# A two-layer decoder step: where the first mixer loads its sample states and exponential table, and the order of the second mixer's weight transposes

## The chip, the cores and the metric

The kernel runs on one core of one Trainium2 chip. The metric is the device time of one execution in microseconds (us); lower is better. The time before is the median of three runs.

## The reference, cut to what matters

One inference step of a two-layer decoder with width 1024 works on a prompt of 1024 tokens and on a group of 8 samples with 4 tokens each (1056 tokens in all). Everything is float32.

```python
# layer 0
proj = rmsnorm(h) @ w_in_a                       # q, k (8 heads x 64), v, o (8 x 128), two gates
h_mix, (c, n, m) = mlstm_chunkwise(q, k, v, ...) # chunks of 128 tokens, state c 64 x 128, n 64, m per head
h = h + (sigmoid(o) * rmsnorm_per_head(h_mix)) @ w_out_a
h = h + square(relu(rmsnorm(h) @ w_up[0])) @ w_down[0]
# layer 1
k, v = rmsnorm(h) @ w_kv                         # 16 heads x 64, samples also read 1024 old rows from a paged cache
z = (q @ k.T) * 64**-0.5 + bias
log1mb = where(mask, log_sigmoid(-z), 0)         # stick-breaking: a = sigmoid(z) * prod of (1 - sigmoid) of later keys
a = exp(where(mask, z + reverse_cumsum(log1mb), -inf))
h = h + (a @ v) @ w_out_b
h = h + square(relu(rmsnorm(h) @ w_up[1])) @ w_down[1]
y = rmsnorm(h)
```

The samples begin their mLSTM from given states; their new states and the prompt's last state are outputs, as are the new keys and values.

## The kernel before, in words

The residual stream `h` stays on the chip, feature by token. A float32 product of the dense layers is made of three products of split operands: a high and a low part each of weights and activations, low by low left out. GpSimd (POOL) splits each 128-column weight panel, SyncE's queue (SP) loads it. The 1056 tokens are three tiles of 352 columns. The program is a row of phases with their own semaphores: constants, embedding, the first mixer (`mixer_a`), output projection and MLP, the second mixer (`mixer_b`), output projection and MLP, the final norm. Each engine's order is written out by hand.

**The first mixer** works on the 8 heads in 4 pairs. For a pair, a list of items (`PLANS[p]`, from `items_of`) sets one order for PE, ACT and DVE: `u` (PE spreads the gate sums over the partitions at L741 and L743; ACT makes decay weights of them with Exp at L908), `k` and `v` (PE transposes, L730, ACT copies the rows, L934), `wsp`, `scores`, `dc` (state additions of the prompt), `out` (the previous pair's heads are transposed back, L723), `num` (numerators, copied by ACT at L944), `dcs` (state additions of the samples). Between the items PE works on thirds of the projection tiles of the next pair (L703 to L705), so many as `FILL` says; for the last pair few are left. An `u` item on PE waits until ACT has made the decay weights of the `u` before it, since both use bank 2.

The loop of ACT over the pairs begins at each pair with the load of the **next** pair's sample states: it waits for the present pair's states to be in, and from pair 1 on also for the stores of the pair before (`state_out`), since the two state tiles alternate. `load_state` then issues two DMAs from ACT's own queue, L871 for the matrices and L872 for the normalisers. Behind the items, `squares(p)` applies Sigmoid to the output gates (L952) and squares the numerators (L959, L960); then ACT issues four stores from its queue (L990 to L993), the last of which writes the samples' normalisers, 4 KB of single elements. In the second item of the next pair `inverse_rms` forms the per-head inverse root with Ln (L964) and Exp (L966). DVE then scales the heads (L1169).

ACT evaluates its functions from a table that must be loaded (`ACT_TABLE_LOAD`). The compiler places a load ahead of a function that the present table lacks. The program asks for the table `natural_log_exp_and_others` by name once, at its start (L2011); the first norm's Ln (L315) and Exp (L318) ran without a load of their own behind it, in the later norms each had one.

**The second mixer** works on 16 heads in 8 pairs, and each pair in 8 slots, one for each prompt tile of 128 queries, from tile 7 down to tile 0 (`TILE_AT`). A tile's keys stand in chunks: for tiles 7 to 4 an upper one (keys from 512 on, `x = 0`) and a lower one (keys 0 to 511, `x = 1`), for tiles 3 to 0 one. For each chunk and head PE makes scores (`z`, L1443 and L1447), ACT the two sigmoids (`gates`, L1627 and L1628), DVE a reversed running product (L1770) and the weights (L1776, `a_ready`). The gates of a tile's first chunk wait until DVE has finished the tile before. Slots 0 and 4 of a pair also hold DVE's chain of the samples (L1782, L1785), ahead of the tile's own.

One slot after a tile, PE transposes its weights in packs of two 128-key blocks with two heads each (L1491), ACT copies a pack to SBUF (L1681), and PE multiplies it with the values into bank 7 (L1536); an odd tile number has an even number of blocks, an even one a last pack of one block. The packs, other transposes (`turn`), the thirds of the next pair's projections (L1427 to L1429) and the quarters of the samples' values (L1550) follow one another as `turns` says; the lower chunk's scores come behind the second turn. ACT reads the turns in the same order, with the upper gates ahead of them. The eight tiles `a` form a ring; ACT may write one again when the pack that reads it last has been transposed.

Of the kernel before, what the change touches and what calls it, by code (L numbers as in the profile page):

```python
# [513 lines left out]
def mixer_a(nc, m, own):  # L514

    HP = HA // 2
# [58 lines left out]
    with ExitStack() as c:  # L575
# [287 lines left out]
        def _(act):  # L863
# [104 lines left out]
            for p in range(HP + 1):  # L968
                if p + 1 < HP:
                    act.wait_ge(state_in, 32 * (p + 1))  # L970
                    if p:
                        act.wait_ge(state_out, 64 * p)
                    load_state(p + 1)
                for i, (x, _) in enumerate(PLANS[p]):
                    if x[0] == "u":
                        decay(x)
                    elif x[0] in ("k", "v"):
                        rows(x)
                    elif x[0] == "num":
                        take(p, x[2])  # L980
                    if i == 1 and p:
                        inverse_rms(p - 1)
                if p < HP:
                    squares(p)
                    act.wait_ge(cs_ready, 3 * p + 3)
                    act.wait_ge(c_ready, NC * p + NC)
# [220 lines left out]
def mixer_b(nc, m, own):  # L1207
# [18 lines left out]

    PACKS = [[(c, min(2, t + 1 - 2 * c)) for c in range(t // 2 + 1)] for t in TILE_AT]
    PACK0 = [sum(len(x) for x in PACKS[:n]) for n in range(SLOTS + 1)]

# [39 lines left out]
    with ExitStack() as c:  # L1269
# [66 lines left out]
        def unit_no(p, n, x, h2):  # L1336

            return 2 * (p * CHUNK0[SLOTS] + CHUNK0[n] + x) + h2
# [74 lines left out]
        def _(pe):  # L1413
# [36 lines left out]

            def turn(y):

                no = TURN_NO[y]
                if no >= 2:

                    pe.wait_ge(turn_read, no - 1)
                bank = m.bank[5 + no % 2]
                kind, p, e = y
                if kind in ("values", "keys"):
# [24 lines left out]
                elif kind == "pack":  # L1484
                    n, c = e
                    if c == 0:
                        pe.wait_ge(a_ready, unit_no(p, n, len(CHUNKS[n]) - 1, 1) + 1)
                    for i in range(PACKS[n][c][1]):
                        for h2 in range(2):
                            col = (2 * i + h2) * P  # L1490
                            last = pe.transpose(bank[:, col:col + P], a_block(p, n, 2 * c + i, h2), m.ident[:, :])  # L1491
# [15 lines left out]
            def follow(y):  # L1507
# [17 lines left out]
                elif kind == "pack":  # L1525
                    n, c = e
                    no, tile = p * PACK0[SLOTS] + PACK0[n] + c, TILE_AT[n]
                    pe.wait_ge(turn_read, TURN_NO[y] + 1)
                    if c == 0 and (p or n):

                        pe.wait_ge(y_ok, p * SLOTS + n)
                    for i in range(PACKS[n][c][1]):
                        kb = 2 * c + i
                        for h2 in range(2):
                            col = (2 * i + h2) * P
                            last = pe.matmul(m.bank[7][hr(h2), 0:P], vrow[p % 2][:, kb, hr(h2)], aT[no % 2][:, col:col + P],  # L1536
                                             start=(kb == 0), stop=(kb == tile), skip_group_check=True)
                    last.then_inc(pv_ready, 1)
# [68 lines left out]
        def _(act):  # L1607
# [5 lines left out]
            def gates(p, n, x):  # L1613
                c0, c1 = CHUNKS[n][x]
                act.wait_ge(z_ready, p * CHUNK0[SLOTS] + CHUNK0[n] + x + 1)
                for h2 in range(2):
                    u, head = unit_no(p, n, x, h2), 2 * p + h2
                    if u >= RING:

                        pu, nu, xu, _ = UNITS[u - RING]  # L1620
                        upper = len(CHUNKS[nu]) > 1 and xu == 0
                        act.wait_ge(turned, TURN_NO["pack", pu, (nu, len(PACKS[nu]) - 1 if upper else min(1, len(PACKS[nu]) - 1))] + 1)
                    if x == 0 and u >= 2:
# [429 lines left out]
```

## Time and profile before

| what | value |
|---|---|
| median of 3 runs | 3212.4 us (3210.67 to 3216.61) |
| the profiled execution's own time | 3212.0 us |
| its span in the profile | 3210.2 us |
| PE busy | 2914.1 us, 91% |
| PE weight loads busy | 2646.6 us, 82% |
| DVE busy | 1363.2 us, 42% |
| ACT busy | 857.8 us, 27% |
| POOL busy | 769.2 us, 24% |
| mean granted clock of PE | 0.956 of full |

The profile is of one execution. Spans of the engines are taken from its records; register, semaphore and DMA-issuing instructions don't count as busy. PE is TensorE, DVE VectorE, ACT ScalarE, POOL GpSimd, SPq and ACTq the queues of SyncE and ScalarE as they issue DMAs. "idle before <-X" says how long an engine stood still ahead of an instruction and what released it; "issue" means that the profile shows no releaser, as in a wait for a DMA's semaphore. The first mixer lies between about 65 and 562 us, the second between about 1450 and 2315 us.

### The profile page before, as it was taken

What the parts mean: (1) busy time and instruction counts of PE and PEld (TensorE: products, weight loads), DVE (VectorE), ACT (ScalarE), POOL (GpSimd) and SP (SyncE); (2) the same over time, 40 slices, a digit from 0 to 9 for tenths busy, and PEclk for the clock granted to TensorE, in tenths of its full rate; (3) what the DMA queues carried; (4) which work ended last, traced back from release to release, by engine and by line L of the source; (5) the groups of instructions that cost most, each with busy time, mean ns of one, the idle gap of its engine ahead of it and who ended that gap; (6) DMA issues with size and microseconds to landing.
All of it is one profiled execution on the core that took longest, in us unless ns stands there. A gap on an engine that the chain in (4) does not pass through costs nothing. (4 is left out here: it accounts for less than half of the span.)

```text
span 3210.2 us, 49314 instructions
## 1 busy us (share of the span) xinstructions
PE 2914.1 (91%) x19749; PEld 2646.6 (82%) x19749; DVE 1363.2 (42%) x1993; ACT 857.8 (27%) x1677; POOL 769.2 (24%) x452
## 2 busy tenths in 40 slices
PE   5979698999999999988988889888799999999996
PEld 4968586989999999976666666666598999999995
DVE  4323233353334444344555554554525433334442
ACT  3111212131011111123545455545503111011114
POOL 3211120323322233331211121110032333322230
PEclk8999897999999999998999999999899999999997
DMA  5664413322222222223333333333411111111111
GB/s 154 189 153 138 87 34 15 107 88 84 91 91 91 91 91 91 91 76 100 110 100 105 106 106 109 97 108 86 148 57 40 47 46 40 45 46 46 46 46 60
DMA packets 362481, 277.66 MB, mean 86 GB/s; under 512 B 31394, under 2 KB 353954, under 8 KB 360290
## 3 DMA queue, kind: packets, MB, share of 16 engines
q1 hardware_dynamic: 341002, 258.18, 27.2%
q10 hardware_dynamic: 21336, 17.47, 2.6%
q8 instruction: 103, 1.69, 0.2%
q14 instruction: 40, 0.33, 0.0%
HBM read 251.58 MB, written 91.11 MB: 107 GB/s over the span
## 5 line engine op out<-in xcount | busy, mean ns | idle before, releaser
L162 POOL CAST w_hi<-w_raw 128x1024 fp32r<-128x1024 f32 x194 | 209.0, 1077 | 1725.7 <-PE bank L214 945.3
L212 PE MATMUL bank<-x_hi,w_hi 128*128 128x352 f32 x1872 | 605.2, 323 | 4.2 <-DVE p_q L1743 4.2
L214 PE MATMUL bank<-x_hi,w_lo 128*128 128x352 f32 x1872 | 602.0, 322 | 0.0
L213 PE MATMUL bank<-x_lo,w_hi 128*128 128x352 f32 x1872 | 601.5, 321 | 0.0
L212 PE MATMUL bank<-p_u_hi,w_hi 128*128 128x352 f32 x1536 | 496.5, 323 | 14.6 <-DVE p_u_lo L1947 14.6
L164 POOL TENSOR_TENSOR w_lo<-w_raw,w_hi 128x1024 fp32r<-128x1024 f32 x194 | 494.5, 2549 | 15.5
L213 PE MATMUL bank<-p_u_lo,w_hi 128*128 128x352 f32 x1536 | 495.5, 323 | 0.0
L214 PE MATMUL bank<-p_u_hi,w_lo 128*128 128x352 f32 x1536 | 495.3, 322 | 0.0
L1955 DVE TENSOR_TENSOR h<-bank,h 128x352 f32<-128x352 f32 x384 | 200.0, 524 | 492.4 <-PE bank L214 492.4
L1915 ACT ACTIVATE p_relu<-bank 128x352 f32<-128x352 f32 x192 | 89.3, 465 | 1042.7 <-PE bank L214 1032.9
L212 PEld LDWEIGHTS bank<-x_hi,w_hi 128*128 128x128 f32 x1872 | 352.0, 188 | 6.2 <-issue 6.0
L213 PEld LDWEIGHTS bank<-x_lo,w_hi 128*128 128x128 f32 x1872 | 353.0, 189 | 0.0
L214 PEld LDWEIGHTS bank<-x_hi,w_lo 128*128 128x128 f32 x1872 | 352.1, 188 | 0.0
L212 PEld LDWEIGHTS bank<-p_u_hi,w_hi 128*128 128x128 f32 x1536 | 288.5, 188 | 18.7 <-issue 18.7
L214 PEld LDWEIGHTS bank<-p_u_hi,w_lo 128*128 128x128 f32 x1536 | 288.6, 188 | 0.0
L213 PEld LDWEIGHTS bank<-p_u_lo,w_hi 128*128 128x128 f32 x1536 | 288.6, 188 | 0.0
L1770 DVE TENSOR_TENSOR_SCAN square<-square,zero 128x512 f32<-128x512 f32 (+5 forms) x192 | 212.4, 1130 | 137.1 <-ACT square L1628 135.3
L1943 DVE TENSOR_TENSOR p_relu<-p_relu,rms_inverse 128x352 f32<-128x352 f32 x192 | 133.3, 694 | 277.6 <-ACT p_relu L1915 277.6
L1945 DVE CAST p_u_hi<-p_relu_sq 128x352 fp32r<-128x352 f32 x192 | 163.1, 849 | 108.5 <-ACT p_relu_sq L1917 108.5
L703 PE MATMUL bank<-x_hi,w_hi 128*128 128x352 f32 x576 | 199.8, 347 | 0.0
L705 PE MATMUL bank<-x_hi,w_lo 128*128 128x352 f32 x576 | 186.5, 324 | 0.0
L704 PE MATMUL bank<-x_lo,w_hi 128*128 128x352 f32 x576 | 186.2, 323 | 0.0
(238 smaller groups left out, 4134.7 us busy)
## 6 DMA issues: line engine op xcount, KB each, us to landing
k_pages<-in_cache_k SPq DMA_DIRECT2D x64, 512.0 KB, 5.5
w_raw<-in_w_up SPq DMA_DIRECT2D x64, 512.0 KB, 4.0
v_pages<-in_cache_v SPq DMA_DIRECT2D x64, 512.0 KB, 4.6
w_raw<-in_w_down SPq DMA_DIRECT2D x64, 512.0 KB, 3.3
p_pages<-k_pages SPq DMA_DIRECT2D x256, 128.0 KB, 2.4
p_pages<-v_pages SPq DMA_DIRECT2D x256, 128.0 KB, 2.3
w_raw<-in_w_in_a SPq DMA_DIRECT2D x26, 512.0 KB, 4.2
h<-h_spill ACTq DMA_DIRECT2D x16, 528.0 KB, 6.5
```

The costliest lines, as they stand in the source:

```text
L162: pool.tensor_copy(m.whi[slot][:, :], m.wraw[slot][:, :]).then_inc(w.hi, 1)
L164: pool.tensor_tensor(m.wlo[slot][:, :], m.wraw[slot][:, :], f32(m.whi[slot][:, :]), ALU.subtract)\
L212: pe.matmul(bank[:, 0:TW], wh, xh, start=(k == 0), stop=False)
L213: pe.matmul(bank[:, 0:TW], wh, xl, start=False, stop=False)
L214: last = pe.matmul(bank[:, 0:TW], wl, xh, start=False, stop=(k == nk - 1))
L703: pe.matmul(bank[:, 0:TW], wh, xh, start=(kk == 0), stop=False)
L704: pe.matmul(bank[:, 0:TW], wh, xl, start=False, stop=False)
L705: last = pe.matmul(bank[:, 0:TW], wl, xh, start=False, stop=(kk == KT - 1))
L1770: dve.tensor_tensor_scan(stick, stick, m.zero[:, 0:1].broadcast_to([P, hi - lo]), sticks[h2][:, hi:hi + 1] if x else 1.0, ALU.mult, ALU.ad ...
L1943: dve.tensor_tensor(relu[t][:, :], relu[t][:, :], m.rs[:, toks], ALU.mult).then_inc(scaled, 1)
L1945: dve.tensor_copy(uhi[:, u, toks], sqr[t][:, :]).then_inc(hi_ready, 1)
L1955: dve.tensor_tensor(ht, m.bank[t][:, 0:TW], ht, ALU.add).then_inc(w.tile_free[t], 1)
```

## The change

In the first mixer, pair 0 still loads the states of pair 1 at its start. The states of pairs 2 and 3 are now loaded by ACT in the middle of pairs 1 and 2, behind the item `("v", p, (1, 2))`, with the same waits. Behind the squares of each pair the kernel asks for the table `natural_log_exp_and_others` by name, ahead of the stores.

In the second mixer a tile's packs are listed from the last keys to the first. The first pack waits for the weights of the upper chunk only, and the pack with `c == 1`, the first that reads the lower chunk, waits for those of the lower. The accumulation in bank 7 starts with the first pack in the list and ends with the last block of the pack `c = 0`. A ring tile of an upper chunk is free after the third pack from the end, that of a lower chunk or of a single chunk after the last.

```diff
--- before.py
+++ after.py
@@ -966,11 +966,9 @@
                 act.activation(ss[:, :, :], ss[:, :, :], ACT.Exp, scale=-0.5).then_inc(r_ready, 1)
 
             for p in range(HP + 1):
-                if p + 1 < HP:
-                    act.wait_ge(state_in, 32 * (p + 1))
-                    if p:
-                        act.wait_ge(state_out, 64 * p)
-                    load_state(p + 1)
+                if p + 1 < HP and p == 0:
+                    act.wait_ge(state_in, 32)
+                    load_state(1)
                 for i, (x, _) in enumerate(PLANS[p]):
                     if x[0] == "u":
                         decay(x)
@@ -980,8 +978,14 @@
                         take(p, x[2])
                     if i == 1 and p:
                         inverse_rms(p - 1)
+                    if x == ("v", p, (1, 2)) and 0 < p < HP - 1:
+
+                        act.wait_ge(state_in, 32 * (p + 1))
+                        act.wait_ge(state_out, 64 * p)
+                        load_state(p + 1)
                 if p < HP:
                     squares(p)
+                    act.preload_act_table_set("natural_log_exp_and_others")
                     act.wait_ge(cs_ready, 3 * p + 3)
                     act.wait_ge(c_ready, NC * p + NC)
                     if p:
@@ -1224,7 +1228,7 @@
     CHUNKS = [[(512, (t + 1) * P), (0, 512)] if t >= 4 else [(0, (t + 1) * P)] for t in TILE_AT]
     CHUNK0 = [sum(len(x) for x in CHUNKS[:n]) for n in range(SLOTS + 1)]
 
-    PACKS = [[(c, min(2, t + 1 - 2 * c)) for c in range(t // 2 + 1)] for t in TILE_AT]
+    PACKS = [[(c, min(2, t + 1 - 2 * c)) for c in range(t // 2, -1, -1)] for t in TILE_AT]
     PACK0 = [sum(len(x) for x in PACKS[:n]) for n in range(SLOTS + 1)]
 
     PACK_AFTER, ROWS_AT = 1, {0: "values", 5: "keys"}
@@ -1448,14 +1452,14 @@
                                          stop=True, skip_group_check=True)
                 last.then_inc(z_ready, 1)
 
-            def turn(y):
-
-                no = TURN_NO[y]
+            def turn(x):
+
+                no = TURN_NO[x]
                 if no >= 2:
 
                     pe.wait_ge(turn_read, no - 1)
                 bank = m.bank[5 + no % 2]
-                kind, p, e = y
+                kind, p, e = x
                 if kind in ("values", "keys"):
                     b0, nb = GROUPS[e]
                     if kind == "values" and e == 0:
@@ -1482,10 +1486,12 @@
                     last = pe.matmul(bank[:, 0:NS], m.identb[:, :], m.new_mask[:, e, :], start=False, stop=True,
                                      skip_group_check=True)
                 elif kind == "pack":
-                    n, c = e
-                    if c == 0:
-                        pe.wait_ge(a_ready, unit_no(p, n, len(CHUNKS[n]) - 1, 1) + 1)
-                    for i in range(PACKS[n][c][1]):
+                    n, y = e
+                    c, blocks = PACKS[n][y]
+                    if y == 0 or c == 1:
+
+                        pe.wait_ge(a_ready, unit_no(p, n, 1 if len(CHUNKS[n]) > 1 and c < 2 else 0, 1) + 1)
+                    for i in range(blocks):
                         for h2 in range(2):
                             col = (2 * i + h2) * P
                             last = pe.transpose(bank[:, col:col + P], a_block(p, n, 2 * c + i, h2), m.ident[:, :])
@@ -1523,18 +1529,19 @@
                                          skip_group_check=True)
                     last.then_inc(zs_done, 1)
                 elif kind == "pack":
-                    n, c = e
-                    no, tile = p * PACK0[SLOTS] + PACK0[n] + c, TILE_AT[n]
+                    n, x = e
+                    c, blocks = PACKS[n][x]
+                    no = p * PACK0[SLOTS] + PACK0[n] + x
                     pe.wait_ge(turn_read, TURN_NO[y] + 1)
-                    if c == 0 and (p or n):
+                    if x == 0 and (p or n):
 
                         pe.wait_ge(y_ok, p * SLOTS + n)
-                    for i in range(PACKS[n][c][1]):
+                    for i in range(blocks):
                         kb = 2 * c + i
                         for h2 in range(2):
                             col = (2 * i + h2) * P
                             last = pe.matmul(m.bank[7][hr(h2), 0:P], vrow[p % 2][:, kb, hr(h2)], aT[no % 2][:, col:col + P],
-                                             start=(kb == 0), stop=(kb == tile), skip_group_check=True)
+                                             start=(x == 0 and i == 0), stop=(c == 0 and i == blocks - 1), skip_group_check=True)
                     last.then_inc(pv_ready, 1)
 
             def values(p, g, quarter):
@@ -1619,7 +1626,7 @@
 
                         pu, nu, xu, _ = UNITS[u - RING]
                         upper = len(CHUNKS[nu]) > 1 and xu == 0
-                        act.wait_ge(turned, TURN_NO["pack", pu, (nu, len(PACKS[nu]) - 1 if upper else min(1, len(PACKS[nu]) - 1))] + 1)
+                        act.wait_ge(turned, TURN_NO["pack", pu, (nu, len(PACKS[nu]) - (3 if upper else 1))] + 1)
                     if x == 0 and u >= 2:
 
                         act.wait_ge(a_ready, u - 1)
```

## Rows read from the trace of the kernel before

**Rows 1.** The page, part 1: busy us, share of the span, instructions.

```profile
PE 2914.1 (91%) x19749; PEld 2646.6 (82%) x19749; DVE 1363.2 (42%) x1993; ACT 857.8 (27%) x1677; POOL 769.2 (24%) x452
```

**Rows 2.** List of waits, 100 to 600 us: who waited for whom, total us, times, longest.

```profile
PE bank L741 <- ACT p_decay_weights L908: 52.6, 5, 24.2
```

**Rows 3.** Timeline, pair 1 to 2: start, length, engine, line, operation, [idle before <-releaser].

```profile
345.70 0.36 ACTq L990 DMA_DIRECT2D out_c_prompt<-p_states  x1
...
347.06 1.62 ACTq L993 DMA_DIRECT2D out_n_sample<-p_state_sample  x1
...
347.31 0.29 ACT L960 ACTIVATE p_squares_sample<-p_numerator 32x128 f32<-32x128 f32 x1
...
370.43 1.73 ACTq L872 DMA_DIRECT2D p_state_sample<-in_state_n  x1
372.24 1.28 ACT L908 ACT_TABLE_LOAD   x1 [24.64 <-issue]
...
374.73 2.07 PE L741 MATMUL bank<-squares,identity 8*128 8x512 f32 x2 [24.19 <-ACT p_decay_weights L908]
...
381.22 1.12 PE L741 MATMUL bank<-squares,identity 8*128 8x512 f32 x2
```

**Rows 4.** Windows, 5 us: busy and count of PE, PEld, DVE, ACT, POOL, PEclk, DMA, GB/s.

```profile
375.00:380.00 5.00, 5.00 (x15) 3.33 (x16) 0.84 (x3) 4.39 (x10) 0.00 (x0) 0.54 0.04 3
```

**Rows 5.** Timeline, pair 0 to 1, engine PE.

```profile
244.87 2.07 PE L741 MATMUL bank<-squares,identity 8*128 8x512 f32 x2 [23.61 <-ACT p_decay_weights L908]
...
251.46 1.12 PE L741 MATMUL bank<-squares,identity 8*128 8x512 f32 x2
...
255.34 1.12 PE L741 MATMUL bank<-squares,identity 8*128 8x512 f32 x2
```

**Rows 6.** Line L993, the store of the sample normalisers: issue to landing.

```profile
DMA to landing us min/median/max: 12.2/19.3/30.0
```

**Rows 7.** List of waits, 1455 to 2400 us.

```profile
PE bank L1491 <- DVE p_weights L1776: 43.0, 9, 6.4
```

**Rows 8.** Timeline, second mixer, slot 1 of pair 1: DVE, ACT, PE.

```profile
1602.68 3.37 DVE L1776 TENSOR_TENSOR p_weights<-p_weights,square 128x511 f32<-128x511 f32 x2
...
1609.55 0.58 ACT L1627 ACTIVATE p_weights<-bank,p_bias 128x384 f32<-128x384 f32 x1 [5.41 <-DVE p_weights L1776]
...
1610.18 1.08 PE L1491 MATMUL bank<-identity,p_weights 128*128 128x128 f32 x4 [5.64 <-DVE p_weights L1776]
...
1610.95 0.59 ACT L1628 ACTIVATE square<-bank,p_minus_bias 128x384 f32<-128x384 f32 x1
...
1616.56 1.13 PE L1443 MATMUL bank<-p_k,p_q 64*128 64x512 f32 x4
```

**Rows 9.** Timeline, pair 2 of the first mixer, engine ACT.

```profile
429.56 0.26 ACT L934 COPY p_v_rows<-bank 32x128 f32<-32x128 f32 x1 [5.52 <-PE bank L730]
447.92 0.87 ACT L944 COPY p_numerator<-bank 128x387 f32<-128x387 f32 x2 [18.10 <-PE bank L818]
```

**Rows 10.** Timeline, pair 2 to 3.

```profile
481.96 0.61 PE L743 MATMUL bank<-causal,identity_bf 128*128 128x512 bf16 x1
...
482.02 1.28 ACT L966 ACT_TABLE_LOAD   x1
...
484.62 2.07 PE L741 MATMUL bank<-squares,identity 8*128 8x512 f32 x2 [1.20 <-ACT p_decay_weights L908]
```

**Rows 11.** Timeline, behind pair 3.

```profile
553.56 1.28 ACT L966 ACT_TABLE_LOAD   x1
```

**Rows 12.** Timeline, entry of the second mixer, ACT and PE.

```profile
1449.71 1.28 ACT L318 ACT_TABLE_LOAD   x1
1451.01 1.08 ACT L318 ACTIVATE rms_inverse<-rms_inverse 128x1056 f32<-128x1056 f32 x1
...
1453.28 0.63 PE L212 MATMUL bank<-x_hi,w_hi 128*128 128x352 f32 x1 [4.18 <-DVE p_q L1743]
```

**Rows 13.** Windows, 2 us, columns as in rows 4, slot 1 of pair 1.

```profile
1612.00:1614.00 2.00, 2.00 (x11) 1.62 (x13) 1.45 (x3) 0.02 (x1) 0.00 (x0) 0.50 0.00 0
```

## The prediction

> **What bounds the kernel now.** I began with the page: PE is busy for 2914.1 us of 3210.2 [rows 1], so nearly everything that can be won is PE's idle time, and what the clock loses behind it. The question for each edit is therefore which of PE's waits it ends, and what stands next in line. The list of waits over the first mixer names one large item: PE waited 52.6 us, in five pieces, for the decay weights that ACT writes at L908 [rows 2]. The timeline of the boundary between pair 1 and pair 2 tells why. ACT finishes the squares of pair 1 at 347.6, issues the stores of the states (the last, L993, at 347.06), and does nothing until 370: its queue stands at the wait for those stores, put ahead of the load of the next states. Then come the load's issues (L872, to 372.16), a table load of 1.28 us, the first decay group, and PE starts at 374.73 after 24.19 us of idleness [rows 3]. PE restarts at the lower clock: granted clock 0.54 in the next 5 us, so close to 1.2 GHz of 2.4 [rows 4]. The boundary between pairs 0 and 1 is the same: 23.61 us idle [rows 5]. What ACT waits for is the store of the sample normalisers, which lands 12.2 to 30.0 us after its issue [rows 6].
>
> The list of waits over the second mixer has one item that is large in each piece: 43.0 us in nine waits of PE's transposes for DVE's products (L1491 on L1776) [rows 7]. Seven of them, one to each of pairs 0 to 6, are 5.5 to 6.4 us long and 40.1 in all; the one of pair 1 stands in the rows [rows 8]. It falls in the slot after tile 7: the first transposes ask for the last chunk, though they are of no use there to the chunk that was ready before.
>
> **First mixer: loads moved to mid stage.** Removed is ACT's wait at the start of pairs 1 and 2; the same wait and the same two DMA issues (the second took 1.73 us of ACT's queue [rows 3]) now stand behind the copy of the last value rows. In pair 2 that copy is at 429.56, and ACT's next work is the copy of the numerators at 447.92 [rows 9]. I cost them at nothing: this gap hides them, and if that cover went the price would be some 2 us, twice. SP's and POOL's queues are not passed. Reached 26 us earlier, without the stall, the wait still comes 56 us after the issue of the stores, against a landing of 30.0 at worst [rows 6]. The states are needed only at the next pair's last numerators.
>
> What is late next at the boundary? ACT's squares end at 347.60, the asked-for table load starts there, and from the start of a table load to PE's restart the row shows 2.49 us (372.24 to 374.73): 350.09. PE wants the decay weights at 374.73 - 24.19 = 350.54 [rows 3]. So the whole wait goes, with 0.45 us to spare. Added to it is the slow restart: from 244.87 to the next pair of L741 matmuls at 251.46 PE took 6.59 us; the stretch after it, 251.46 to 255.34, has the same fifteen projection matmuls and three 128-wide transposes fewer, and took 3.88 [rows 5]. With these I estimate 4.2, so 2.4 us are given back; the second boundary's stretch is 374.73 to 381.22, 6.49, so 2.3 [rows 3]. The bounds are zero and, if everything scaled by 2.07 to 1.12 as L741 itself did, 3.0. Sum: 23.6 + 2.4 + 24.2 + 2.3 = **52.5 us**.
>
> **First mixer: the table asked for by name.** Sigmoid throws out the table that holds exp and ln together; until now exp, ln and exp then each got a load of 1.28 us. One load per pair replaces three. At boundaries 1 and 2 the second and third load lay beside PE's restart, and are in the sum above. At boundary 3 (no state wait) the load before the exponential of the head norm runs from 482.02, and the second decay group can't start before its end at 483.3, while PE's matmul for it ended at 482.57; PE's wait of 1.20 at 484.62 shrinks by that 0.8 [rows 10]. Lower bound: nothing; upper: the whole 1.2. After pair 3 the chain is serial (sums, ln, load, exp, heads scaled, PE), and the load at 553.56 lies on it: **1.3 us** [rows 11]. The new load takes the place of one that stood hidden before the ln. Behind this, the joint table should still be in place at the second mixer's norm, as Relu, Square and Copy never called for another: there the load of 1449.71 ends, the exp at 1451.01 follows, DVE waits for it and PE for DVE (4.18 us) [rows 12]: 1.3 us, or nothing if the tracking of the table stops at the loop of the MLP. In the first MLP PE has the whole first panel to work through before ACT and DVE can be late, so nothing is won. Sum: 0.8 + 1.3 + 1.3 = **3.4 us**.
>
> A load's price is its 1.28 us: the exp of 1451.01 started 0.02 us after the load's end [rows 12]. The Trainium skill (ScalarE: Activation LUTs, What ACT_TABLE_LOAD costs) puts a drain of about 1.38 us on top, 2.66 for each switch, and by this the part would be worth some 3 us more, less about 2 us of new wait at boundary 2. The trace shows no such drain, and I go by the row.
>
> **Second mixer: transposes from the last keys.** In the slot after tile 7 the first transposes will ask for the upper chunk alone. DVE finished that at 1602.68 + 3.37 = 1606.05; they started at 1610.18, behind the lower chunk [rows 8]. So PE starts 4.0 us earlier. It can't use more than it is fed: the next scores (L1443, at 1616.56) need the scores' banks read by ACT, whose gates of the next tile wait for the lower chunk as before (5.41 us, from 1609.55) and end at 1610.95 + 0.59 = 1611.54 [rows 8]. PE's work in between took 6.38 us at a granted clock of 0.5 [rows 13]; at the full clock, which a gap of 1.5 us should not cost it, some 4.2 us, so it is through at 1610.3 and waits about 1.2 us for the gates. The scores start at 1611.6 in place of 1616.56: 4.96 us. For seven pairs **34.7 us**. The bounds: nothing if a copy is late each time, and 7.8 (5.64 and half of the slow 4.4) if ACT could follow. I take the time of the gates, since both ends of it stand in rows. The other slots keep their lengths: no such wait stands there, and the last pair has no projections and no long wait. The one-block pack of an odd tile comes first instead of last; its copy is at most 0.3 us longer to wait for, behind page and sample transposes; nothing. The ring of weight buffers asks for transposes of the slot before, long done.
>
> **Sum.** 52.5 + 3.4 + 34.7 = 90.6 us off the profiled execution's own 3212.0 (span 3210.2): 3121.4; the runs' median is 0.4 higher, so 3121.8, and I say 3122.
>
> **Rivals.** (1) *The table load holds up ACT's queue.* The stores are issued behind it then, not beside the squares: from L990 at 345.70 to the end of L993 at 348.68 are 3.0 us [rows 3]. The load ends at 348.9, the decay group comes at 351.9, PE restarts at 353.1 against 350.54: 2.5 us lost at boundary 2, and some 1.7 at boundary 3, where PE is idle already. At boundary 1 PE comes later. That gives 3126. For it: no table load of before is followed by an issue. Against it: issues ran beside activations freely. Chance 0.17.
> (2) *Second mixer, the wait only changes its name.* PE gets its transposes, then stands behind ACT, which copies them only after the gates; if pages or copies cost another 3 to 4 us there, each pair gives 1 to 1.5 us: about 3122 + 25 = 3147. Against it are the times above. Chance 0.12.
> (3) *The request is not honoured*, and loads are still placed before exp and ln: four loads more, one of them in the 0.45 us of slack at boundary 2, none of the 3.4 gained: 3127. The table asked for at the program's start did serve the first norm's ln and exp, hence 0.04.
> (4) *Slower.* The stores of the states land so late that ACT stands at the wait in mid stage, and PE at the numerators. It starts to cost at a landing of 56 + 18 = 74 us and makes the kernel slower only from about 74 + 91/2, some 120 us, against 30.0 seen [rows 6, 9]: something above 3212. Chance 0.01.
> The forecast has 0.66. A change under 0.2% (6 us, about what a measurement of this kernel can tell from none) would need both large parts to fail: 0.01.
>
> **Range.** Below, the restarts at their upper bound and a few us of each pair's remaining 1.2 us: 3112. Above, rival 2 and most of rival 1: 3148.
>
> **What would show it.** ACT's long wait before L908 and PE's 52.6 us for it shrink to a few us; loads at L908, L964 and L966 are gone and four stand behind the squares, with the issue of L990 beside or behind them (rival 1); the state loads stand behind L934 in mid stage. In the second mixer nine waits of 43.0 become waits of 1.5 us at the transposes and about 1.2 at L1443, with the granted clock at 1.0 through them; a pair gets about 5 us shorter. I am wrong if the boundaries show a new wait of PE over 3 us, or the time per pair moves by under 3.

## The result, and the profile after

The changed kernel took 3130.4 us in the median of four runs (3125.4 to 3132.2), the kernel before 3211.5 on the same chip. The ratio is 0.974 (95% interval 0.9725 to 0.9759), so 81 us or 2.6% came off. The profiled execution took 3130.8 us with a span of 3129.0, so 81.2 us came off the span. The forecast was 3122, with 90.6 us off.

The page, part 1, of the changed kernel (answers to [rows 1]). PE is busy for 17.8 us less with the same 19749 matmuls, so 17.8 of the 81.2 us came from a higher clock and the other 63 from idle time:

```profile
PE 2896.3 (93%) x19749; PEld 2632.3 (84%) x19749; DVE 1362.9 (44%) x1993; ACT 842.5 (27%) x1666; POOL 768.2 (25%) x452
```

**First mixer.** The list of waits from 100 to 560 us (answers to [rows 2]) has 3.8 us where 52.6 stood:

```profile
PE bank L723 <- DVE p_numerator L1173: 6.9, 1, 6.9
PE bank L741 <- ACT p_decay_weights L908: 3.8, 3, 2.4
```

The boundary between pair 1 and pair 2, timeline of ACT and PE (answers to [rows 3, 4]; start, length, engine and line). The stores L994 to L997 are issued beside the squares, the last at 324.17, and ACT's queue doesn't stop behind them. The load asked for by name follows the last square, and the first decay group follows the load:

```profile
322.81 0.36 ACTq L994 DMA_DIRECT2D out_c_prompt<-p_states  x1
...
322.92 1.09 PE L741 MATMUL bank<-squares,identity 8*128 8x512 f32 x2 [0.80 <-DVE p_state_sample L1151]
...
324.17 1.81 ACTq L997 DMA_DIRECT2D out_n_sample<-p_state_sample  x1
...
324.42 0.29 ACT L960 ACTIVATE p_squares_sample<-p_numerator 32x128 f32<-32x128 f32 x1
...
324.73 1.28 ACT L988 ACT_TABLE_LOAD   x1
...
326.09 1.14 ACT L908 ACTIVATE p_decay_weights<-bank,p_gate_columns 128x128 f32<-128x128 f32 x4
...
327.60 1.12 PE L741 MATMUL bank<-squares,identity 8*128 8x512 f32 x2
...
331.79 1.12 PE L741 MATMUL bank<-squares,identity 8*128 8x512 f32 x2
```

PE doesn't wait for ACT here any more: between the L741 groups at 322.92 and 327.60 it has work, and the next group comes 4.19 us behind the one at 327.60. Before, the group at 374.73 stood behind the stall, and the same 23 matmuls from there to the next group took 6.49 us [rows 3]. That the stall was the wait for the stores can be read from the trace before: the last store landed at 241.20 and at 369.94, and the state loads were issued at 241.27 and 370.01. The states of the next pair are loaded 56 us later, right behind the copy of the last value rows (answers to [rows 9]). The issue starts 0.06 us after the copy does, so the wait for the stores had ended by then; the copy of the numerators comes 18 us later:

```profile
380.15 0.26 ACT L934 COPY p_v_rows<-bank 32x128 f32<-32x128 f32 x1 [5.52 <-PE bank L730]
380.21 0.39 ACTq L871 DMA_DIRECT2D p_state_sample<-in_state_c  x1
380.63 1.37 ACTq L872 DMA_DIRECT2D p_state_sample<-in_state_n  x1
398.51 0.87 ACT L944 COPY p_numerator<-bank 128x387 f32<-128x387 f32 x2 [18.10 <-PE bank L818]
```

**Second mixer.** The list of waits from 1398.6 to 2235.8 us (answers to [rows 7]): the transposes wait 15.2 us instead of 43.0, the scores 11.4 instead of 2.9.

```profile
PE bank L1543 <- ACT p_weights_t L1688: 24.0, 28, 2.1
PE bank L1557 <- DMA p_pages<-v_pages: 17.2, 17, 2.6
PE bank L1497 <- DVE p_weights L1783: 15.2, 8, 2.9
PE bank L1478 <- ACT p_page_keys_t L1676: 11.9, 9, 1.5
PE bank L1447 <- ACT square L1635: 11.4, 11, 1.6
```

Slot 1 of pair 1, timeline (answers to [rows 8]). The scores at 1554.50 follow the start of the transposes by 5.40 us instead of 6.38, and the wait ahead of the transposes is 1.67 instead of 5.64. Without the new wait of 1.20 ahead of the scores, the 39 matmuls in between took 4.20 us instead of 6.38:

```profile
1549.10 0.63 PE L1497 MATMUL bank<-identity,p_weights 128*128 128x128 f32 x4 [1.67 <-DVE p_weights L1783]
...
1552.45 0.58 ACT L1634 ACTIVATE p_weights<-bank,p_bias 128x384 f32<-128x384 f32 x1 [5.43 <-DVE p_weights L1783]
...
1553.86 0.59 ACT L1635 ACTIVATE square<-bank,p_minus_bias 128x384 f32<-128x384 f32 x1
...
1554.50 1.13 PE L1447 MATMUL bank<-p_k,p_q 64*128 64x512 f32 x4 [1.20 <-ACT square L1635]
```

And the windows of the same place (columns as in [rows 4, 13]); the clock that was 0.50 there is 1.00:

```profile
1551.00:1553.00 2.00, 2.00 (x28) 1.71 (x26) 2.00 (x4) 0.55 (x2) 0.00 (x0) 1.00 0.03 8
```

Cut at the first matmul of each phase, the profiled executions have these stages (us). "Second mixer" runs from PE's wait at L212 for its first panel to the output projection's last wait at L241; it holds the same 6265 matmuls in each kernel:

| kernel | first mixer | MLP and norm | second mixer | PE busy in it | PE idle by waits in it |
|---|---|---|---|---|---|
| before | 500.02 | 887.93 | 863.11 | 750.77 | 108.2 |
| changed | 445.94 | 885.12 | 837.15 | 740.86 | 92.4 |
| change | -54.1 | -2.8 | -26.0 | -9.9 | -15.8 |

These are 82.9 us; the start-up took 2.3 us longer in this execution and the last MLP 0.6 less, which makes the span's 81.2. The first mixer did what was forecast; the second fell short. A pair of it, from its first scores to those of the next, went from 105.7 to 102.3 us in the median, 3.4 and not 4.96 us shorter.

One execution of each is a rough measure. The second mixer of before took 857.2 to 863.1 us in the four profiled executions that have it or its long waits (the kernel before is the longest), and the changed one 833.6 to 837.2 in three. The last pair, which has no long wait, alone lay between 82.1 and 86.3. The seven pairs with the long wait, from the first scores of pair 0 to those of pair 7, took 739.6 to 743.8 us with it (743.5 in the kernel before) and 716.1 to 716.7 without: 27.3 us between the two kernels, where 34.7 were forecast.

The windows show something new in its later slots. In pair 2, in the slot after tile 6, PE waits 1.45 us for ACT's copy of a page (1672.0 to 1673.5), and behind this wait comes a stretch at the lower clock. Timeline and windows of the changed kernel:

```profile
1669.35 1.13 PE L1447 MATMUL bank<-p_k,p_q 64*128 64x512 f32 x4
...
1673.47 0.88 PE L1478 MATMUL bank<-identity,p_pages 128*128 128x128 f32 x4 [1.45 <-ACT p_page_keys_t L1676]
...
1688.28 0.66 PE L1543 MATMUL bank<-p_weights_t,p_v_rows 128*64 128x128 f32 x8 [1.97 <-ACT p_weights_t L1688]
```

```profile
1671.00:1673.00 2.00, 1.02 (x9) 0.61 (x8) 1.18 (x1) 2.00 (x5) 0.00 (x0) 1.00 0.30 88
1673.00:1675.00 2.00, 1.53 (x12) 1.20 (x12) 2.00 (x4) 1.49 (x3) 0.00 (x0) 0.69 0.15 43
1675.00:1677.00 2.00, 2.00 (x12) 1.57 (x9) 0.46 (x1) 0.51 (x1) 0.00 (x0) 0.50 0.45 131
```

Read in windows of 1.7 us over the first seven pairs, the kernel before has a low stretch of 6.8 us behind each of the seven long waits and three of 3.4 us elsewhere; the changed kernel has none behind those waits and six of 3.4 us in later slots. Two gaps stand there in every pair of the changed kernel: 1.45 us at the page transposes in the slot after tile 6, and 1.97 us at the values in the slot after tile 5. Three of its low stretches follow the first and three the second, never both in one pair. In the kernel before the first of these gaps was 1.24 us and was never followed by a low stretch; two of its three followed the gap of 1.97, the third a wait of 1.79 us for value pages.

### The profile page after: what moved, and what is told of

The parts are those of the page before. It is cut to its first block and busy times, and to the rows that moved or that the text cites. A ratio compares the mean times of both kernels' runs of the same rounds, so it can differ in the third digit from the quotient of the medians.

```text
span 3129.0 us, 49335 instructions
## 1 busy us (share of the span) xinstructions
PE 2896.3 (93%) x19749; PEld 2632.3 (84%) x19749; DVE 1362.9 (44%) x1993; ACT 842.5 (27%) x1666; POOL 768.2 (25%) x452
## 5 line engine op out<-in xcount | busy, mean ns | idle before, releaser
L162 POOL CAST w_hi<-w_raw 128x1024 fp32r<-128x1024 f32 x194 | 208.7, 1076 | 1672.0 <-PE bank L214 945.4
L212 PE MATMUL bank<-x_hi,w_hi 128*128 128x352 f32 x1872 | 605.2, 323 | 2.9 <-DVE p_q L1750 2.9
L212 PE MATMUL bank<-p_u_hi,w_hi 128*128 128x352 f32 x1536 | 496.4, 323 | 14.6 <-DVE p_u_lo L1954 14.6
L212 PEld LDWEIGHTS bank<-x_hi,w_hi 128*128 128x128 f32 x1872 | 352.1, 188 | 4.9 <-issue 4.7
L212 PEld LDWEIGHTS bank<-p_u_hi,w_hi 128*128 128x128 f32 x1536 | 288.5, 188 | 18.8 <-issue 18.8
```

Of the source, the lines that this page charges most:

```text
L162: pool.tensor_copy(m.whi[slot][:, :], m.wraw[slot][:, :]).then_inc(w.hi, 1)
L212: pe.matmul(bank[:, 0:TW], wh, xh, start=(k == 0), stop=False)
```

## The experiments

### Each part alone

First: do the parts add up, and which falls short? `a_states_only` is the kernel before with the moved loads, `a_table_only` the kernel before with the request, `b_only` the changed kernel with the first mixer of before.

```diff
 # a_states_only: as the first two hunks of the change, without this line; a_table_only: this line alone
                     squares(p)
+                    act.preload_act_table_set("natural_log_exp_and_others")
 # b_only: the hunks from PACKS on
```

> The kernel before with the state loads moved to mid stage alone; no table is asked for, the second mixer as before. My sum: the two boundaries lose their 24.2 and 23.6 us of idleness and 4.7 us of slow restart, but three table loads per pair stay, one ahead of the first decay group of the next pair and two ahead of the second. The boundary behind pair 2, which never had the state wait, shows what that costs: PE waits 2.6 and 1.2 us. So 52.5 less 2 x 1 to 2 x 4: 44 to 51 us faster, 3161 to 3168. The rival, that the store's landing moves to another wait (mid stage, DVE's wait before the states), gives under 30 us and a wait of that name.

> The kernel before with the table asked for by name alone; state loads and second mixer as before. At the two boundaries with the state wait the loads lie behind that wait: the first decay group comes 1.3 us earlier (its load now stands ahead of the wait), the second group 2.6 us earlier beside PE's restart. With the 0.8, 1.3 and 1.3 us of my sum: 3.4 to 10 us faster, 3202 to 3208. Rival: the compiler goes on placing loads, then 4 loads more and the same time or 1 to 2 us slower; the trace would show loads at L908, L964 and L966.

> The second mixer's change alone, first mixer as before. In the profile of the changed kernel the second mixer is 26.0 us shorter, where I had forecast 34.7. If the parts are independent: 24 to 29 us faster, 3183 to 3188, and in each pair a fall of the granted clock in slots 2 to 4. If the shortfall came from the first mixer's part (pages or clock shifted by it), this kernel gives the forecast 34.7: 3177.

| kernel | median, us | ratio to before (interval) |
|---|---|---|
| a_states_only | 3157.2 | 0.983 (0.9814 to 0.9847) |
| a_table_only | 3207.9 | 0.9986 (0.9973 to 0.9998) |
| b_only | 3186.4 | 0.9921 (0.9903 to 0.9938) |

Beside them the kernel before took 3211.5. So alone the parts give 54.2, 3.6 and 25.0 us: 82.8 in sum, where the whole gave 81. By the intervals these are 49 to 60, 0.6 to 8.7 and 20 to 31 us. The 34.7 forecast for the second mixer lie outside, so its shortfall is there without the other parts too. `a_table_only` and `b_only` came out as expected, but for the fall of the clock, which six of the seven pairs of `b_only` have. `a_states_only` was 4 us faster than its range: the three loads that stay at each boundary were to cost PE 1 to 4 us, and its new waits for decay weights at the two boundaries are 0.91, 0.71 and 0.37 us; the rest of the difference is within its interval.

Between the two edits of the first mixer the split is less plain than the sum. By stages (one profiled execution each) its length is 500.0 before, 453.1 with the states, 500.4 with the table and 445.9 with both (445.7 to 447.9 in all eight executions that have both). Of the 7.2 us between 453.1 and 445.9 the request took 4.3 off PE's waits, as the waits of `a_states_only` from 65.4 to 518.5 us show against the 6.9 and 3.8 above. The other 2.9 are PE's busy time (428.4 against 425.5 us), which differs by more between two executions of one code: the first mixer of before took 500.0 us in the kernel before and 506.3 in `b_only`, with PE busy for 429.6 and 436.8. For the same reason the 500.4 of `a_table_only` don't say that the request is worth nothing there; PE's waits were 2.3 us shorter than in the kernel before. The lines of `a_states_only`:

```profile
PE bank L723 <- DVE p_numerator L1172: 8.2, 1, 8.2
PE bank L741 <- ACT p_decay_weights L908: 6.8, 6, 2.6
```

### Why a pair gains less than 5 us

Two theories. The first: the one-block pack of an even tile, now the first, is too short a piece for ACT's copy to hide behind, and costs in slots 2, 4 and 6. The second: with the stall at the boundary gone, the clock falls at a shorter gap later in the pair. `b_full_first` takes the upper packs in ascending order, then the lower ones, so that no short pack comes first. `b_order_only` keeps the new order and waits for all of the tile's weights, as before. `b_thirds_later` moves the thirds of the projections behind the lower chunk's scores in every slot that has them.

```diff
 # b_full_first
-range(t // 2, -1, -1)
+[*range(2, t // 2 + 1), *range(min(2, t // 2 + 1))]
-if y == 0 or c == 1:
+if y == 0 or c == 0:
 # b_order_only
-pe.wait_ge(a_ready, unit_no(p, n, 1 if len(CHUNKS[n]) > 1 and c < 2 else 0, 1) + 1)
+pe.wait_ge(a_ready, unit_no(p, n, len(CHUNKS[n]) - 1, 1) + 1)
 # b_thirds_later
                     turn(y)
-                    if fill:
-                        third(p, d)
-                        d, fill = d + 1, fill - 1
                     if i == 1 and lower:
                         z(p, n, 1)
+                    if fill and (i or not lower):
+                        third(p, d)
+                        d, fill = d + 1, fill - 1
```

> The changed kernel with the packs of the upper chunk in rising order and then those of the lower chunk in rising order: the upper chunk is still first and the early start at the boundary stays, but the one-block pack of an even tile is no longer the first. Theory 1 (my forecast's failed term is the one-block pack first: PE has half a pack less to do before it stands behind ACT's gates, idles 1.45 us in place of 1.24, and the granted clock falls): the idle goes back to 1.24, no clock fall in slot 2, 1.3 us a pair come back: 8 to 10 us faster than the changed kernel, about 3121. Theory 2 (the clock falls once a pair anyway in slots 2 to 4, whatever the pack order, now that it no longer falls at the boundary): within 3 us of the changed kernel, 3127 to 3131.

> The changed kernel with the new order of packs, but the first pack waits for both chunks again, as before. The wait of 5.5 us per pair at the first transposes comes back in both theories. Theory 1: the order itself costs, so the second mixer is slower than in the kernel before, by up to 1.3 us a pair: 36 us above the changed kernel, about 3165, with a clock fall in slot 2 as well as at the boundary. Theory 2: the second mixer is as long as before (863 us), 26 us above the changed kernel, about 3156, and no clock fall in slots 2 to 4 except the one or two that the kernel before had.

> The changed kernel with PE's order in the slots of tiles 7 to 4 altered: the lower chunk's scores come right behind the second turn, and the thirds of the projections start behind them instead of ahead, so ACT's gates of the lower chunk run beside a third. Where PE stands behind ACT's gates (about 1.45 and 1.97 us in slots 2 and 3, 1.2 in slot 1) it now has a third of 1.0 to 1.5 us to do. If these waits and the clock that falls behind them are what is left: 2 to 5 us a pair, 14 to 35 us faster, 3095 to 3116. Rival: DVE reads a projection tile later and its lower chain, in order behind that, comes later: the wait moves to the transposes of the next slot and nothing is won, or up to 10 us lost.

`b_full_first`: 3128.5 us, ratio 0.9746 (0.9725 to 0.9767), second mixer 836.2 us, and seven low stretches of 3.4 us, one to a pair, each behind the gap of 1.97 us. The gap at the page transposes is still 1.45 us in each pair, though no short pack comes first. The first theory is out. `b_order_only`: 3153.7 us, ratio 0.9833 (0.9807 to 0.9858). That is the first mixer's part alone (3211 less 57.8 is 3153.2), so the order by itself gives nothing and costs little (the page transposes wait 1.45 us instead of 1.24 in each pair, as in every kernel that takes the upper chunk first and keeps both thirds ahead), and within this all of the 23.3 us to the changed kernel comes from asking for the upper chunk only. Its seven stretches of 6.8 us behind the long waits are back, and none is left in the later slots, with the order of the packs the same and both later gaps still there. In pair 2 its gap is as long as the changed kernel's, and the clock stays at 1.00 behind it (timeline of PE, and window):

```profile
1682.80 0.65 PE L1478 MATMUL bank<-identity,p_pages 128*128 128x128 f32 x4 [1.46 <-ACT p_page_keys_t L1676]
```

```profile
1683.00:1685.00 2.00, 2.00 (x20) 1.49 (x18) 1.79 (x3) 1.15 (x3) 0.00 (x0) 1.00 0.16 46
```

So what brings the later stretches is not the gap's extra 0.2 us and not the order of the packs, but that the stall at the boundary is gone: with it there were 0, 0, 2 and 3 stretches of 3.4 us in the first seven pairs (`a_states_only`, `b_order_only`, `a_table_only`, before), without it 6, 6, 6 and 7 (changed, `after_again`, `b_only`, `b_full_first`). A pair is also 3 us shorter without the stall, and by what path the earlier stall keeps the clock up later these runs don't show.

`b_thirds_later`: 3127.9 us, ratio 0.9748 (0.9725 to 0.977), no gain, as its rival had it, though the wait went to another place than the rival said. The wait at the transposes nearly vanished, and its time stands at the scores, the longest 3.6 us; the low stretch (3.4 us, seven times) now follows this one. Its list of waits, 1396.6 to 2229.9 us:

```profile
PE bank L1447 <- ACT square L1635: 50.6, 32, 3.6
PE bank L1543 <- ACT p_weights_t L1688: 13.9, 36, 2.1
PE bank L1528 <- ACT p_page_keys_t L1676: 10.0, 16, 0.7
PE bank L1557 <- DMA p_pages<-v_pages: 6.6, 12, 2.7
PE bank L1497 <- DVE p_weights L1783: 4.5, 2, 3.8
```

A third between the upper and the lower scores is what hides ACT's upper gates, and without one PE waits up to 3.6 us there. So one third belongs ahead of the lower scores and the other behind.

### Closing the later gaps

In the slots after tiles 6 and 5 there are two thirds; in the changed kernel both lie ahead of the lower scores. `b_split_thirds` puts the second behind them, in these two slots alone; `after_again` is the changed kernel on the same chip.

```diff
                     turn(y)
+                    ahead = i == 1 and lower and n in (2, 3)
+                    if ahead:
+                        z(p, n, 1)
                     if fill:
                         third(p, d)
                         d, fill = d + 1, fill - 1
-                    if i == 1 and lower:
+                    if i == 1 and lower and not ahead:
                         z(p, n, 1)
```

> The changed kernel; in the slots after tiles 6 and 5 alone, the scores of the lower chunk now stand ahead of the second third of a projection tile instead of behind it, so that this third (1.7 us of TensorE) lies beside ACT's gates. My theory: in the changed kernel a gap of 1.45 us (page transposes waiting for ACT's page copy behind the gates) or 1.97 us (values waiting for the weight copy) in these slots is followed by 3.4 us at the lower clock in each pair, and this eats 1.7 us of the pair's gain. If so, both gaps close here, the spells in these slots go, and with 1.5 to 2 us of each gap the pair gets 3 to 5 us shorter: 15 to 35 us under the changed kernel, some 3095 to 3115. Rival: the wait only moves, as it did with the thirds put later in all slots (TensorE then waits at the scores for the upper gates, and the low clock turns up elsewhere): 3124 to 3132.

> The changed kernel itself, for a comparison on the same chip: 3125 to 3133 by every theory, with one spell of low clock to a pair in the second mixer.

`b_split_thirds` took 3106.5 us, ratio 0.9675 (0.9651 to 0.9699); `after_again` 3130.5, ratio 0.9751 (0.9727 to 0.9776). So 24 us more came off, and this is the fastest of the kernels. Its list of waits over the second mixer, 1402.1 to 2209.7 us:

```profile
PE bank L1543 <- ACT p_weights_t L1691: 14.9, 33, 2.1
PE bank L1497 <- DVE p_weights L1786: 14.2, 8, 2.9
PE bank L1557 <- DMA p_pages<-v_pages: 14.1, 16, 2.3
PE bank L1447 <- ACT square L1638: 12.0, 10, 2.6
```

The wait for the page copy fell from 11.9 us to 1.8 and is not among these, that for the transposed weights fell from 24.0 to 14.9, and nothing took their place. The same slot of pair 2 now runs without a gap (timeline of PE and ACT). The scores stand ahead of the third, so ACT's gates end at 1665.3 beside it and the page copy of 1665.21 is done before PE asks for its bank:

```profile
1661.74 1.13 PE L1447 MATMUL bank<-p_k,p_q 64*128 64x512 f32 x4
...
1664.64 0.70 ACT L1638 ACTIVATE square<-bank,p_minus_bias 128x511 f32<-128x511 f32 x1
...
1665.21 0.60 ACT L1679 COPY p_page_keys_t<-bank 128x512 f32<-128x512 f32 x1
...
1665.87 0.66 PE L1478 MATMUL bank<-identity,p_pages 128*128 128x128 f32 x4
```

Its windows there:

```profile
1664.00:1666.00 2.00, 2.00 (x17) 1.43 (x16) 1.78 (x2) 1.89 (x5) 0.00 (x0) 1.00 0.03 9
1666.00:1668.00 2.00, 1.96 (x20) 1.55 (x20) 1.85 (x3) 1.25 (x3) 0.00 (x0) 1.00 0.59 167
```

A pair takes 98.1 to 98.6 us, and two low stretches of 3.4 us are left in the first seven pairs. The whole second mixer, in one window of each kernel, changed first and then `b_split_thirds`:

```profile
1398.60:2235.80 837.20, 740.86 (x6265) 551.31 (x6265) 447.18 (x568) 437.05 (x916) 131.66 (x67) 0.96 0.37 105
```

```profile
1402.10:2209.70 807.60, 733.50 (x6264) 545.80 (x6265) 457.00 (x568) 437.99 (x916) 136.00 (x67) 0.98 0.38 108
```

It is 29.6 us shorter: PE's waits fell by 22.8 (92.4 to 69.6), its busy time by 7.4. (The other stages of this execution were 4 us longer than in the changed kernel's, within what they differ from kernel to kernel.)

Last, each slot alone, to see which gap brings the low stretch.

```diff
-                    ahead = i == 1 and lower and n in (2, 3)
+                    ahead = i == 1 and lower and n == 2    # b_split_slot2; b_split_slot3 has n == 3
```

> The changed kernel with the scores of the lower chunk ahead of the second third in the slot after tile 6 alone. Moved in both slots this gave 24 us over the changed kernel: gaps for 13 to 16 of these, low clock for the rest. Theory (either gap is enough to bring the spell of lower clock, and there is one to a pair): the gap of 1.45 us closes, 7 x 1.45 = 10 us, but the gap of 1.97 us in the next slot stays and now brings the spell in each pair: some 3120 (3117 to 3123), spells still one to a pair. Rival (the 1.45 us gap is what brings the spell): 10 + 7 x 1.7 = 22 us, about 3109, and no spells.

> The same in the slot after tile 5 alone. Theory: the gap of 1.97 us closes, 7 x 1.7 to 2 = 12 to 14 us, the gap of 1.45 us stays and keeps the spell: 3116 to 3119, spells one to a pair. Rival (the 1.97 us gap is what brings the spell): about 3105, no spells. If both slots give 10 to 14 us by themselves with one spell to a pair, the clock was no part of the 24 us of both.

They took 3116.9 us (0.9705, 0.9688 to 0.9723) and 3117.4 us (0.9707, 0.9689 to 0.9725): 13.5 and 13.1 us off the changed kernel's 3130.5. Together that is 26.6, and both at once gave 24. By time, slot 3 came out as its theory said and slot 2 within 0.1 us of it. But the reason given, that the gap which is left keeps a stretch in every pair, was wrong: low stretches in the first seven pairs numbered six in the changed kernel, four with slot 2, six with slot 3 and two with both, and the two effects add. With slot 2 three of the four follow the gap of 1.97 us that is left. With slot 3 only one of the six follows the gap of 1.45 us that is left; three stand at the transposes of slot 1 and two behind waits for value pages. The windows of the two kernels over the second mixer, slot 2 first:

```profile
1399.20:2221.60 822.40, 737.56 (x6264) 548.21 (x6265) 449.98 (x568) 437.83 (x916) 131.36 (x67) 0.97 0.37 106
```

```profile
1398.80:2222.30 823.50, 739.25 (x6265) 550.20 (x6265) 457.01 (x568) 436.63 (x916) 138.09 (x67) 0.97 0.37 106
```

PE's busy time fell by 3.3 and 1.6 us, and by 7.4 with both. The waits fell by 12.5 in each (to 79.9). So most of these 24 us were plain waits of PE, and the clock was about a quarter.

## Why the prediction was right, and where it fell short

**The states: right.** ACT's stall of 24 us before the load went, PE's waits at L741 went from 52.6 to 3.8 us, and nothing new stands at the boundary. The two parts inside the first mixer were forecast at 52.5 + 0.8 + 1.3 = 54.6 us and measured 54.1. The cover named for the moved issues held: they cost ACT nothing (380.21, above) and PE nothing. The stretches behind the two restarts were to shrink to 4.2 us each: 6.59 became 4.21 (224.32 to 228.53) and 6.49 became 4.19 (327.60 to 331.79).

**The table: right in each wait that was named.** The wait of 1.20 at boundary 3 [rows 10] became 0.38, against 0.8 forecast; the wait at L723 behind pair 3 went from 8.2 to 6.9 (1.3 forecast); the entry of the second mixer from 4.18 [rows 12] to 2.90 (1.3 forecast). Rows of the changed kernel for the first and the last:

```profile
434.24 2.07 PE L741 MATMUL bank<-squares,identity 8*128 8x512 f32 x2 [0.38 <-ACT p_decay_weights L908]
```

```profile
1396.36 1.08 ACT L318 ACTIVATE rms_inverse<-rms_inverse 128x1056 f32<-128x1056 f32 x1
...
1398.64 0.63 PE L212 MATMUL bank<-x_hi,w_hi 128*128 128x352 f32 x1 [2.90 <-DVE p_q L1750]
```

The request was honoured, so rival 3 is out: no load stands at L908, L964 or L966, and four stand at L988. The MLP's stage was another 1.5 us shorter than the entry explains; no wait of PE in it accounts for that, and over the twelve profiled executions it lay between 885.0 and 888.9 us, so that is no finding.

**Rival 1 is out.** The stores were issued at 322.81 to 324.17, beside the squares, and the load came behind them at 324.73 though it stands ahead of them in the program. Whether a load would hold up an issue that becomes ready behind it, no run tried.

**The drain.** The prediction went by the row and not by the drain that the Trainium skill (ScalarE: Activation LUTs, What ACT_TABLE_LOAD costs) adds to a load. The trace after agrees with the row: the load of 324.73 starts 0.02 us after the last square's end (324.71), and the decay group starts at 326.09, 0.08 after the load's end. Behind 25 of the 29 loads of this execution the next activation starts 0.01 us after the load's end.

**The second mixer: right in mechanism, a term mis-sized.** Forecast 34.7 us, measured 26 in the profile and 25.0 alone. At the boundary itself each step came as written: transposes' waits of 1.66 (2.40 in pair 0), then 1.20 for the gates, and the work between them took 4.20 us at the full clock, where 4.2 were forecast. Over the two lines PE's waits fell from 45.9 to 26.6 us, 19.3, where the forecast held 7 x (5.64 - 1.64 - 1.20) = 19.6. Rival 2, a new wait in place of the old one, is out at this place. What failed is the step "The other slots keep their lengths", and the clock with it:

- The remaining 34.7 - 19.6 = 15.1 us were to come from the work behind the wait running at 2.4 and not 1.2 GHz. PE's busy time fell by 9.9. The 6.8 us at low clock behind each long wait went, but six stretches of 3.4 us came in later slots. The prediction wrote that a gap of 1.5 us should not cost PE its clock, which held at the changed kernel's boundaries and not in the slots behind them. Gaps of 1.24 and 1.97 us had stood there before too; in seven pairs only three low stretches came, two of them behind the gap of 1.97. This takes 5.2 us. An estimate agrees: `b_split_thirds` has four stretches fewer than the changed kernel, and PE's busy time in the seven pairs is 5.5 us less (640.5 against 646.0), 1.4 for each, so three more cost about 4.2.
- Other waits grew: for the value pages from 14.1 to 17.2, for the page copies from 10.2 to 11.9, while that for the transposed weights fell from 25.3 to 24.0. This takes 3.5 us. The page copies' part is the 0.2 us in each pair that the order of the packs brings. That the value pages are waited for because PE comes to them earlier is likely and was not tested.

Together 8.7 us, which is 34.7 less the 26.0 measured in one execution of each; other pairs of executions give 20.0 (`b_order_only` to changed) to 29.5 us (before to `b_only`) in place of the 26.0. The prediction had put the changed place of the one-block pack at nothing (it calls it the pack of an odd tile; it is that of an even one), and `b_full_first` bears this out. That the low stretches follow the gaps is shown as far as `b_order_only` (boundary wait back, the same later gaps, later stretches gone), `b_thirds_later` (the longest gap at another place, the stretches behind it) and `b_split_thirds` (gaps closed, four of six stretches gone, 24 us won) can show it. Which gap is answered by a stretch in a given pair stays open: the two single slots left four and six, not one to a pair.

## What to carry to other kernels

When a wait for the last of several products is taken away, follow the time through the whole period, not only to the next wait: here gaps that had cost only their own length were followed by the lower clock once that stall was gone. Place filler work so that each of two dependent waits has some (one third ahead of the lower scores, one behind); moving all of it to one side only renames the wait. A load that waits for stores of single elements belongs where the queue is empty anyway, and a table that serves two functions should be asked for by name once behind the function that throws it out (here 0.6 to 8.7 us for 11 loads fewer).

## What the runs showed that was not expected

The kernel before kept a granted clock of 1.00 behind a wait of 1.24 us at the page transposes of pair 2 (its timeline and windows):

```profile
1738.82 0.66 PE L1474 MATMUL bank<-identity,p_pages 128*128 128x128 f32 x4 [1.24 <-ACT p_page_keys_t L1669]
```

```profile
1739.00:1741.00 2.00, 2.00 (x20) 1.51 (x19) 1.81 (x3) 1.15 (x3) 0.00 (x0) 1.00 0.15 42
```

The changed kernel fell to 0.50 behind one of 1.45 us at the same place. The 0.2 us between the gaps are not the reason, since `b_order_only` kept 1.00 behind the longer one in all seven pairs (above). What these two kernels have and the changed one lacks is the long stall some 23 us earlier. So the same wait can be free or cost the clock, and which it was went here with another wait well ahead of it.
